# Two layers on one core: the first two columns of two projections made in turn, and two of the last four down blocks of the first MLP turned back by VectorE

## The chip, the core and the metric

The kernel runs on one core of a Trainium2 chip. A core has a matrix engine (TensorE, PE in the profile, with its weight loads as PEld), a vector engine (VectorE, DVE), a scalar engine (ScalarE, ACT), GpSimd (POOL), and DMA queues, here issued by SyncE (SP). The engines run their own instruction streams and meet at semaphores. The metric is the device time of one execution in microseconds; lower is better.

## The reference, cut to what matters

256 tokens of width 2048 pass through two layers, all in float32. Layer 1 is a Mamba-2 branch and an attention branch, whose outputs are joined and projected, and an MLP with squared ReLU. Layer 2 is an attention branch of three kinds and a gated delta rule, merged by two gates, projected, and a second MLP.

```python
def hybrid_layer_2(x, ...):
    ...
    g_a, g_b = jnp.split(jax.nn.sigmoid(merge), 2, axis=-1)
    x = x + (g_a * (o_a @ w_pa) + g_b * (o_b @ w_pb)) @ w_o
    h = rms_norm(x, ln2_w)
    return x + jnp.square(jax.nn.relu(h @ w_up)) @ w_down
```

In layer 1 the output projection is a product of 2048 inputs, half of them attention (`w_out_att`) and half the gated, normed output of the state-space part (`w_out_ssd`); its MLP has the same form as the last line above, with 8192 hidden units.

## The kernel before

**Weights.** They stream from HBM in pieces of 128x2048 through a ring of four. Each piece is two units of 128x1024. ScalarE casts a unit to its high half (`w_hi`, `unit_hi`), VectorE takes the difference (`w_lo`, `unit_lo`), and there is room for four units (`UNITS`). ScalarE may cast a unit once TensorE has used the one four back (`unit_used`). `weight_order` lists the pieces; the pieces of a pair of columns made in turn are split as first half, first half, second half, second half (`turns`, `unit_order`).

**Columns.** Most projections keep x transposed (features by tokens) and make 128 output features, a column, at a time: k tiles of 128 inputs, for each a 512-wide product of the high weights with both halves of x and a 256-wide one of the low weights with the high half of x. `project` makes columns one after another, `column` takes k tiles in twos (`products_of_two`, lines 548 and 551), `column_pair` makes two columns in turn (lines 542 and 543 in `products`). Three banks of PSUM go round: `bank_free` waits until the bank's last user but two has been read (`bank_read`), column by column.

**The joined output of layer 1.** `project_out_att` makes the 16 columns A0 to A15 over the attention half, 8 k tiles each, while VectorE works on the gate; then 16 columns G0 to G15 over the gated half follow. VectorE adds each bank to x in two halves (`residual`, lines 1349 and 1352). The gated half comes in four pairs of tiles; line 1651 makes the low half of each (semaphore `gate_dve`), steps lo00, lo01, lo10 and lo11.

**The MLPs.** They are made by tokens: `up_blocks` and `down_blocks` make 128 tokens by 512 features in a bank (lines 558 to 560), for four quarters f of the hidden units with four blocks n each, eight units a block. VectorE turns the squared ReLU with 32x32 block transposes (`turn_up`, line 1675), and adds the down blocks in `x_toks` (line 1775). In the first MLP's last quarter TensorE turns each finished block back to features (`turned_back`, line 850, eight transposes of 128x128 in two banks, in the middle of the next block), VectorE adds it to x (`back_to_x`, line 1719), ScalarE and VectorE make the gained x for the next layer (`gained`, line 1360), and GpSimd adds squares (line 2857). In the second MLP's first quarter VectorE turns x to tokens (`turn_x`, line 1683).

**The merged output of layer 2.** The last merge columns are multiplied and added by VectorE (lines 1977 and 1981); ScalarE casts a pair of tiles (`merged_split`, line 2676) and VectorE makes its low half (line 1954, semaphore `merged_lo`), eight pairs in all. Then `project` makes the 16 columns W0 to W15 of `w_o`, 16 k tiles each.

Of the kernel before, what the change touches and what calls it, by code (L numbers as in the profile page):

```python
# [13 lines left out]
P = 128  # L14
D = 2048
# [204 lines left out]
def weight_order(t):  # L220
# [4 lines left out]
    def add(name, first, n, in_turns=False):  # L225
        if in_turns:
            turns.append(len(order))
        order.extend(t[name][first + i] for i in range(n))
# [38 lines left out]
    merge(MERGE_BEHIND)  # L267
    add("w_o", 0, KD)
    mlp("w_up2", "w_down2")
# [16 lines left out]
def build(nc, t_in, x_out, bias_rows, x_kept, decays_kept):  # L286
    with ExitStack() as ctx:
# [6 lines left out]
        def sem(name):  # L294
            return ctx.enter_context(nc.semaphore(name))
# [220 lines left out]
        merged_hi, merged_lo = sem("merged_hi"), sem("merged_lo")  # L516
        tok_turned = sem("x_turned")
        down_made, down_added = sem("down_first_tokens_made"), sem("down_added")
# [16 lines left out]
        def _(e):  # L535
# [304 lines left out]
            A = GATE["dve"]  # L840
            drain(project(KD, mix, 0, 8, (gate_dve, [A[f"lo{k // 4}{k // 2 % 2}"] for k in range(8)])))

# [37 lines left out]
            def down_blocks(m, f, hid):  # L880
# [3 lines left out]
                for n in range(D // BLOCK):  # L884
                    b = (4 * m + f) * (D // BLOCK) + n
                    back = m == 0 and f == 3
                    last = m == 1 and f == 3 and n == 3
                    if back and n >= 2:
                        e.wait_ge(back_added, 2 * (n - 1))
                    for k in range(KD):  # L890
                        if back and n > 0 and k == 8:
                            turned_back(n - 1)
                        if n == 0 and k % 4 == 0:
# [362 lines left out]
            drain(merge(MERGE_BEHIND))  # L1256
            drain(project(KD, hn2, 0, KD, (merged_lo, [k // 2 + 1 for k in range(KD)])))
            mlp(1, mix2, hn2)
# [5 lines left out]
        def _(e):  # L1264
# [429 lines left out]
            def up_blocks(m, f, hid):  # L1694
                nonlocal unit
                for n in range(D // BLOCK):
                    b = (4 * m + f) * (D // BLOCK) + n
                    for i in range(8):
# [10 lines left out]
                        if n > 0:  # L1709
                            if i in (1, 2):  # L1710
                                turn_up(b - 1, i - 1)
                            elif i == 4:
                                squared_lo(b - 1, hid)

            def back_to_x(n):
                b = 3 * (D // BLOCK) + n
                for half in range(2):
                    e.wait_ge(back_turned, 2 * n + half + 1)
                    e.tensor_tensor(pair(xT, 2 * n + half), pair(xT, 2 * n + half), psum[3 + 2 * (b % 2) + half][:, :],
                                    ALU.add).then_inc(back_added, 1)  # L1720

# [12 lines left out]
            def down_blocks(m, f, hid):  # L1734
                nonlocal unit
                for n in range(D // BLOCK):
                    b = (4 * m + f) * (D // BLOCK) + n
                    for i in range(8):
# [9 lines left out]
                        if m and f == 0 and n > 0 and i in range(2, 6):  # L1748
                            turn_x(n, i - 2)
                        if m == 0 and f == 3 and n > 0:  # L1750
                            if i == 5:
                                back_to_x(n - 1)
                            elif i > 5:
                                for t in range(4 * n + 2 * i - 16, 4 * n + 2 * i - 14):
                                    gained(t, "ln1", mix2)
# [381 lines left out]
            e.wait_ge(x_back, 32)  # L2137
            drain(project(16, 2, gained_residual("ln2", mix2)))
            mlp(1, hn2)
# [5 lines left out]
        def _(e):  # L2145
# [81 lines left out]

            def project_gathered(per_use, gain=None, dst=None):

# [8 lines left out]

                for t in range(KD):
                    for i in range(per_use):  # L2240
                        split_to(unit + UNITS)
                        unit += 1
                        if i == per_use - 1:
                            if t > 0:
                                finish(t - 1, use - 1)
                            if t == KD - 1:
                                finish(t, use)
                            use += 1
                        yield
# [577 lines left out]
            merged_split(7)  # L2827
            drain(project_gathered(2, "ln2", mix2))
            mlp(1, hn2)
# [265 lines left out]
```

## Time and profile before

| | |
|---|---|
| median of 3 runs | 2618.96 us (2618.95 to 2619.89) |
| the profiled execution's own time | 2619.45 us |
| its span, first to last instruction | 2617.6 us |
| mean granted clock of TensorE | 0.999 of full speed |
| TensorE busy | 2600.3 us |
| VectorE, ScalarE, GpSimd busy | 1864.2, 1307.9, 212.9 us |

The span lies inside the time; 1.85 us are around it. A share of busy time is an average over the whole program. What an edit is worth is read from the place where it is made: which engine waits there, and for what.

### The profile page before, as it was taken

Reading aid. Unit: us, or ns where it says so; the run is one execution under the profiler, and the core shown is the slowest. Engines: PE = TensorE matmul, PEld = TensorE weight load, DVE = VectorE, ACT = ScalarE, POOL = GpSimd, SP = SyncE. Lnnn points to the kernel's source line nnn. Section 1 sums busy time; section 2 is a strip of 40 time slices with the busy share of each in tenths; the row PEclk is TensorE's granted clock in tenths of the full one; section 3 lists DMA queues with packets and bytes.
Section 4 is the critical chain, followed back from the end, with each engine's and each line's share of the span. In section 5 each row is a group of like instructions: output and inputs, shape, how many; then the busy total and the mean of one; then the engine's idle time right before and its main releaser. Section 6 shows DMA issues by size and latency. Waiting matters only on the chain. (4 is left out here: it accounts for less than half of the span.)

```text
span 2617.6 us, 33824 instructions
## 1 busy us (share of the span) xinstructions
PE 2600.3 (99%) x13404; PEld 2207.0 (84%) x13404; DVE 1864.2 (71%) x2717; ACT 1307.9 (50%) x1823; POOL 212.9 (8%) x188
## 2 busy tenths in 40 slices
PE   9999999999999999999999999999999999999998
PEld 8788888888888888888888888888888888888887
DVE  7788797757658567786877767566678877585685
ACT  6545554534445345565555545455554354453453
POOL 4014010000000000130412300000100000000000
PEclk9999999999999999999999999999999999999999
DMA  7654555555555555576444333355555555555553
GB/s 266 164 216 167 188 177 184 202 193 188 199 189 181 209 191 195 181 264 235 145 146 144 114 128 129 129 211 178 206 196 204 194 184 204 184 186 209 187 199 129
DMA packets 68468, 483.87 MB, mean 185 GB/s; under 512 B 8039, under 2 KB 8183, under 8 KB 11224
## 3 DMA queue, kind: packets, MB, share of 16 engines
q1 hardware_dynamic: 65520, 467.43, 50.4%
q0 software_dynamic: 2272, 12.87, 1.7%
q8 instruction: 106, 1.74, 0.3%
q10 hardware_dynamic: 520, 1.43, 0.1%
q14 instruction: 50, 0.41, 0.0%
HBM read 475.38 MB, written 6.31 MB: 184 GB/s over the span
## 5 line engine op out<-in xcount | busy, mean ns | idle before, releaser
L1280 DVE TENSOR_TENSOR w_lo<-weight_ring,w_hi 128x1024 fp32r<-128x1024 f32 x882 | 1083.6, 1239 | 577.8 <-ACT w_hi L2158 573.7
L2158 ACT CAST w_hi<-weight_ring 128x1024 fp32r<-128x1024 f32 x884 | 917.1, 1048 | 713.6 <-PE bank L560 580.1
L548 PE MATMUL bank<-mix,w_hi 128*128 128x512 f32 x1776 | 566.8, 400 | 3.1 <-DVE mix L1651 1.2
L558 PE MATMUL bank<-w_hi,h 128*128 128x512 f32 x1056 | 411.7, 390 | 0.0
L558 PE MATMUL bank<-w_hi,mix 128*128 128x512 f32 x1056 | 411.2, 389 | 0.0
L559 PE MATMUL bank<-w_lo,h 128*128 128x512 f32 x1056 | 410.9, 389 | 0.0
L559 PE MATMUL bank<-w_lo,mix 128*128 128x512 f32 x1056 | 410.9, 389 | 0.0
L560 PE MATMUL bank<-w_hi,h 128*128 128x512 f32 x1056 | 410.9, 389 | 0.0
L560 PE MATMUL bank<-w_hi,mix 128*128 128x512 f32 x1056 | 410.8, 389 | 0.0
L551 PEld LDWEIGHTS bank<-mix,w_lo 128*128 128x128 f32 x1776 | 333.6, 188 | 78.7
L551 PE MATMUL bank<-mix,w_lo 128*128 128x256 f32 x1776 | 349.7, 278 | 0.0
L548 PE MATMUL bank<-h,w_hi 128*128 128x512 f32 x864 | 280.6, 406 | 0.0
L548 PEld LDWEIGHTS bank<-mix,w_hi 128*128 128x128 f32 x1776 | 271.4, 189 | 6.5 <-issue 1.7
L1675 DVE STREAM_TRANSPOSE arena<-arena 32x256 f32<-32x256 f32 x512 | 223.0, 436 | 24.1 <-ACT arena L2478 16.9
L558 PEld LDWEIGHTS bank<-w_hi,h 128*128 128x128 f32 x1056 | 198.2, 188 | 41.9 <-DVE w_lo L1280 0.7
L560 PEld LDWEIGHTS bank<-w_hi,mix 128*128 128x128 f32 x1056 | 198.2, 188 | 41.2
L560 PEld LDWEIGHTS bank<-w_hi,h 128*128 128x128 f32 x1056 | 198.2, 188 | 41.2
L559 PEld LDWEIGHTS bank<-w_lo,h 128*128 128x128 f32 x1056 | 198.2, 188 | 41.1 <-issue 0.2
L558 PEld LDWEIGHTS bank<-w_hi,mix 128*128 128x128 f32 x1056 | 198.2, 188 | 40.9
L559 PEld LDWEIGHTS bank<-w_lo,mix 128*128 128x128 f32 x1056 | 198.3, 188 | 40.9
L551 PEld LDWEIGHTS bank<-h,w_lo 128*128 128x128 f32 x864 | 162.3, 188 | 38.2
L551 PE MATMUL bank<-h,w_lo 128*128 128x256 f32 x864 | 170.2, 278 | 0.0
(377 smaller groups left out, 1998.4 us busy)
## 6 DMA issues: line engine op xcount, KB each, us to landing
weight_ring<-in_w_up SPq DMA_DIRECT2D x128, 1024.0 KB, 4.8
weight_ring<-in_w_down SPq DMA_DIRECT2D x128, 1024.0 KB, 4.8
weight_ring<-in_w_merge SPq DMA_DIRECT2D x32, 1024.0 KB, 4.7
weight_ring<-in_w_gdn SPq DMA_DIRECT2D x24, 1024.0 KB, 4.8
weight_ring<-in_w_papb SPq DMA_DIRECT2D x16, 1024.0 KB, 4.8
weight_ring<-in_w_o SPq DMA_DIRECT2D x16, 1024.0 KB, 4.8
weight_ring<-in_w_xbc SPq DMA_DIRECT2D x12, 1024.0 KB, 4.8
weight_ring<-in_w_q SPq DMA_DIRECT2D x8, 1024.0 KB, 4.8
```

The source lines that it names most:

```text
L548: e.matmul(bank[:, :], w_hi[:, unit_at % UNITS, o + j * P:o + (j + 1) * P], x[:, :, at + j * S:at + (j + 1) * S], start=first and j == 0, ...
L551: done = e.matmul(bank[:, 0:S], w_lo[:, unit_at % UNITS, o + j * P:o + (j + 1) * P], x[:, 0, at + j * S:at + (j + 1) * S], start=False, st ...
L558: e.matmul(out, x[:, 0, at:at + m], hi, start=first, stop=False)
L559: e.matmul(out, x[:, 0, at:at + m], lo, start=False, stop=False)
L560: return e.matmul(out, x[:, 1, at:at + m], hi, start=False, stop=last)
L1280: e.tensor_tensor(w_lo[:, i, :], ring[:, p % PIECES, half * UNIT:(half + 1) * UNIT], w_hi[:, i, :].bitcast(F32), ALU.subtract).then_inc(un ...
L1675: done = e.transpose(dst[:, :, :, 32 * r:32 * r + 32], src[:, :, :, 32 * q:32 * q + 32])
L2158: e.copy(w_hi[:, i, :], ring[:, p % PIECES, half * UNIT:(half + 1) * UNIT]).then_inc(unit_hi, 1)
```

## The change

Three places are edited. (A) G0 and G1 are made in turn, four k tiles of each at a time, after both banks and both weight units have been waited for. (B) In the first MLP's last quarter the first and second blocks are turned back by VectorE in 32x32 pieces (`turn_back`) into `turned_m`, in the first units of the next block; the third and fourth still by TensorE. (C) W0 and W1 are made by `column_pair`, two k tiles of each at a time, their pieces split in turn; VectorE and ScalarE read both columns once both are done.

```diff
@@ -265,7 +265,7 @@
     add("w_gz1", 0, 4)
     merge(MERGE_BEFORE)
     merge(MERGE_BEHIND)
-    add("w_o", 0, KD)
+    add("w_o", 0, KD, True)
     mlp("w_up2", "w_down2")
     return order, turns
 
@@ -514,7 +514,7 @@
         head_scaled, z_silu = sem("head_scaled"), sem("z_silu")
         merge_tanh, merge_mult, merge_gated = sem("merge_tanh"), sem("merge_multiplied"), sem("merge_gated")
         merged_hi, merged_lo = sem("merged_hi"), sem("merged_lo")
-        tok_turned = sem("x_turned")
+        tok_turned, back_made = sem("x_turned"), sem("down_blocks_turned")
         down_made, down_added = sem("down_first_tokens_made"), sem("down_added")
         back_turned, back_added = sem("down_turned_back"), sem("down_added_to_x")
         tok_squared, tok_gained, ln_loaded = sem("tokens_squared"), sem("tokens_gained"), sem("ln_rows_loaded")
@@ -838,7 +838,22 @@
                                     together(ssd_output(0), ssd_output(1)), ssd_gate()),
                   one_after_another(project(XBC_T + Z_T, hn), project_out_att()))
             A = GATE["dve"]
-            drain(project(KD, mix, 0, 8, (gate_dve, [A[f"lo{k // 4}{k // 2 % 2}"] for k in range(8)])))
+            gated = [A[f"lo{k // 4}{k // 2 % 2}"] for k in range(8)]
+            banks = []
+            for _ in range(2):
+                banks.append(bank_free())
+                use += 1
+            e.wait_ge(unit_lo, unit + 2)
+            for g in range(2):
+                for j in range(2):
+                    for k in range(4 * g, 4 * g + 4, 2):
+                        if j == 0:
+                            e.wait_ge(gate_dve, gated[k])
+                        done = products_of_two(banks[j], unit + j, k * P, mix, k * S, k == 0, k == 6)
+                    if g == 1:
+                        done.then_inc(unit_used, 1)
+            unit += 2
+            drain(project(KD - 2, mix, 0, 8))
 
             def turned_back(n):
                 b = 3 * (D // BLOCK) + n
@@ -883,13 +898,10 @@
                 nonlocal unit
                 for n in range(D // BLOCK):
                     b = (4 * m + f) * (D // BLOCK) + n
-                    back = m == 0 and f == 3
                     last = m == 1 and f == 3 and n == 3
-                    if back and n >= 2:
-                        e.wait_ge(back_added, 2 * (n - 1))
                     for k in range(KD):
-                        if back and n > 0 and k == 8:
-                            turned_back(n - 1)
+                        if m == 0 and f == 3 and n == 3 and k == 8:
+                            turned_back(2)
                         if n == 0 and k % 4 == 0:
                             e.wait_ge(up_lo, b + k // 4 + 1)
                         if k % 2 == 0:
@@ -1254,7 +1266,8 @@
             drain(delta_chain(0), delta_chain(1), one_after_another(rounds(NORM_TURNS[1]), vector_norms(1)),
                   one_after_another(gdn_projections(1), merge(MERGE_BEFORE)))
             drain(merge(MERGE_BEHIND))
-            drain(project(KD, hn2, 0, KD, (merged_lo, [k // 2 + 1 for k in range(KD)])))
+            column_pair(hn2, (merged_lo, [k // 2 + 1 for k in range(KD)]), 2)
+            drain(project(KD - 2, hn2))
             mlp(1, mix2, hn2)
             assert unit == UNIT_AT["end"] and use == USE["end"]
 
@@ -1712,12 +1725,27 @@
                             elif i == 4:
                                 squared_lo(b - 1, hid)
 
+            def turn_back(n, q):
+
+                b = 3 * (D // BLOCK) + n
+                if q == 0:
+                    e.wait_ge(down_added, 2 * (b + 1))
+                for r in range(4):
+                    src = x_toks[32 * r:32 * r + 32, :].rearrange("p (c n t w) -> p n t c w", c=2, n=D // BLOCK, t=4)
+                    dst = turned_m[n % 2][32 * q:32 * q + 32, :].rearrange("p (t c w) -> p t c w", t=4, c=2)
+                    done = e.transpose(dst[:, :, :, 32 * r:32 * r + 32], src[:, n, :, :, 32 * q:32 * q + 32])
+                done.then_inc(back_made, 1)
+
             def back_to_x(n):
                 b = 3 * (D // BLOCK) + n
                 for half in range(2):
-                    e.wait_ge(back_turned, 2 * n + half + 1)
-                    e.tensor_tensor(pair(xT, 2 * n + half), pair(xT, 2 * n + half), psum[3 + 2 * (b % 2) + half][:, :],
-                                    ALU.add).then_inc(back_added, 1)
+                    if n < 2:
+                        e.wait_ge(back_made, 4 * (n + 1))
+                        got = pair(turned_m[n % 2], half)
+                    else:
+                        e.wait_ge(back_turned, 2 * (n - 2) + half + 1)
+                        got = psum[3 + 2 * (b % 2) + half][:, :]
+                    e.tensor_tensor(pair(xT, 2 * n + half), pair(xT, 2 * n + half), got, ALU.add).then_inc(back_added, 1)
 
             def scaled_tokens(c):
                 last = D // BLOCK - 1
@@ -1748,6 +1776,8 @@
                         if m and f == 0 and n > 0 and i in range(2, 6):
                             turn_x(n, i - 2)
                         if m == 0 and f == 3 and n > 0:
+                            if i in range(1, 5) and n <= 2:
+                                turn_back(n - 1, i - 1)
                             if i == 5:
                                 back_to_x(n - 1)
                             elif i > 5:
@@ -2135,7 +2165,14 @@
             drain(merge(MERGE_BEHIND))
             merged_split(7)
             e.wait_ge(x_back, 32)
-            drain(project(16, 2, gained_residual("ln2", mix2)))
+            evacuate = gained_residual("ln2", mix2)
+            split_to(unit + UNITS + 2)
+            unit += 4
+            e.wait_ge(unit_used, unit)
+            for t in range(2):
+                evacuate(t, psum[use % 3], bank_read[use % 3])
+                use += 1
+            drain(project(KD - 2, 2, lambda t, bank, read: evacuate(t + 2, bank, read)))
             mlp(1, hn2)
             assert unit == made == UNIT_AT["end"] and use == USE["end"]
 
@@ -2225,7 +2262,7 @@
                         e.wait_ge(res_gathered, FOLDED * n_gathered + s - 2)
                 e.activation(dst, pair(xT, s), ACT.Square).then_inc(res_squared, 1)
 
-            def project_gathered(per_use, gain=None, dst=None):
+            def project_gathered(per_use, gain=None, dst=None, paired=False):
 
                 nonlocal unit, use, n_gathered
 
@@ -2236,7 +2273,12 @@
                     if t % 2:
                         gather(t // 2)
 
-                for t in range(KD):
+                if paired:
+                    split_to(unit + UNITS + 2)
+                    unit += 4
+                    use += 2
+                    finish(0, use - 2)
+                for t in range(2 if paired else 0, KD):
                     for i in range(per_use):
                         split_to(unit + UNITS)
                         unit += 1
@@ -2825,7 +2867,7 @@
                   one_after_another(gdn_projections(1), merge(MERGE_BEFORE)))
             drain(merge(MERGE_BEHIND))
             merged_split(7)
-            drain(project_gathered(2, "ln2", mix2))
+            drain(project_gathered(2, "ln2", mix2, paired=True))
             mlp(1, hn2)
             for c in range(2):
                 squares(D // BLOCK - 1, c)
```

**TensorE at A.** The first rows of G0 before; bank2 and bank0 are the banks of G0 and G1, the semaphores are those of `gate_dve`, `unit_lo` and `bank_read`.

```order
L548 MATMUL bank2<-mix,w_hi 128x512 [waits ssd_gate_dve,unit_lo_made,gemm_bank_read2]
L548 MATMUL bank2<-mix,w_hi 128x512
L551 MATMUL bank2<-mix,w_lo 128x256 x2
L548 MATMUL bank2<-mix,w_hi 128x512 [waits ssd_gate_dve]
L548 MATMUL bank2<-mix,w_hi 128x512
L551 MATMUL bank2<-mix,w_lo 128x256 x2
L548 MATMUL bank2<-mix,w_hi 128x512 [waits ssd_gate_dve]
```

The same place in the changed kernel.

```order
L548 MATMUL bank2<-mix,w_hi 128x512 [waits unit_lo_made,ssd_gate_dve,gemm_bank_read0,gemm_bank_read2]
L548 MATMUL bank2<-mix,w_hi 128x512
L551 MATMUL bank2<-mix,w_lo 128x256 x2
L548 MATMUL bank2<-mix,w_hi 128x512 [waits ssd_gate_dve]
L548 MATMUL bank2<-mix,w_hi 128x512
L551 MATMUL bank2<-mix,w_lo 128x256 x2
L548 MATMUL bank0<-mix,w_hi 128x512 x2
L551 MATMUL bank0<-mix,w_lo 128x256 x2
L548 MATMUL bank0<-mix,w_hi 128x512 x2
L551 MATMUL bank0<-mix,w_lo 128x256 x2
L548 MATMUL bank2<-mix,w_hi 128x512 [waits ssd_gate_dve]
```

Four k tiles of G1 have moved between k tiles 3 and 4 of G0, and the first matmul now waits for two banks.

**VectorE at B.** After the adds of the first block (L1775), before.

```order
L1775 TENSOR_TENSOR arena<-arena,bank 128x512 [waits down_added,unit_used]
L1280 TENSOR_TENSOR w_lo<-weight_ring,w_hi 128x1024 [waits unit_hi_made] x6
L1719 TENSOR_TENSOR arena<-arena,bank 128x512 [waits down_turned_back] x2
L1280 TENSOR_TENSOR w_lo<-weight_ring,w_hi 128x1024 [waits unit_hi_made]
L1360 SCALAR_TENSOR_TENSOR h<-arena,vecs,h 128x256 [waits gained_x_hi] x2
```

The same place in the changed kernel, where those lines are 1805, 1293, 1748 and 1373.

```order
L1805 TENSOR_TENSOR arena<-arena,bank 128x512 [waits down_added,unit_used]
L1293 TENSOR_TENSOR w_lo<-weight_ring,w_hi 128x1024 [waits unit_hi_made] x2
L1736 STREAM_TRANSPOSE arena<-arena 32x8x32 [waits down_added]
L1736 STREAM_TRANSPOSE arena<-arena 32x8x32 x3
L1293 TENSOR_TENSOR w_lo<-weight_ring,w_hi 128x1024 [waits unit_hi_made]
L1736 STREAM_TRANSPOSE arena<-arena 32x8x32 x4
L1293 TENSOR_TENSOR w_lo<-weight_ring,w_hi 128x1024 [waits unit_hi_made]
L1736 STREAM_TRANSPOSE arena<-arena 32x8x32 x4
L1293 TENSOR_TENSOR w_lo<-weight_ring,w_hi 128x1024 [waits unit_hi_made]
L1736 STREAM_TRANSPOSE arena<-arena 32x8x32 x4
L1293 TENSOR_TENSOR w_lo<-weight_ring,w_hi 128x1024 [waits unit_hi_made]
L1748 TENSOR_TENSOR arena<-arena 128x512 [waits down_blocks_turned] x2
```

Sixteen transposes stand between the weight splits of the second to fifth unit, and the add-back reads no bank.

**TensorE at C.** In the changed kernel, where the second half of W0 and then of W1 begins (bank1 and bank2 are their banks).

```order
L542 MATMUL bank2<-mix,w_hi 128x512
L543 MATMUL bank2<-mix,w_lo 128x256
L542 MATMUL bank1<-mix,w_hi 128x512 [waits unit_lo_made,merged_lo]
L543 MATMUL bank1<-mix,w_lo 128x256
L542 MATMUL bank1<-mix,w_hi 128x512
L543 MATMUL bank1<-mix,w_lo 128x256
L542 MATMUL bank2<-mix,w_hi 128x512 [waits unit_lo_made]
```

W1's ninth k tile, which waits for the fourth unit, comes two k tiles after W0's ninth; in the kernel before all of W0 stood ahead of W1's first.

## Rows read from the trace of the kernel before

**Rows 1.** The page, part 1: busy time, its share, instructions.

```profile
PE 2600.3 (99%) x13404; PEld 2207.0 (84%) x13404; DVE 1864.2 (71%) x2717; ACT 1307.9 (50%) x1823; POOL 212.9 (8%) x188
```

**Rows 2.** The waits of TensorE: total us, times, longest us.

```profile
PE bank L548 <- DVE mix L1651: 1.2, 1, 1.2
PE bank L548 <- DVE arena L1352: 1.0, 1, 1.0
PE bank L548 <- DVE mix L1954: 0.9, 1, 0.9
```

**Rows 3.** Timeline of PE, 353 to 361: start us, us, line, operation, idle before.

```profile
354.01 0.63 PE L548 MATMUL bank<-mix,w_hi 128*128 128x512 f32 x2
...
356.74 0.73 PE L548 MATMUL bank<-mix,w_hi 128*128 128x512 f32 x2 [1.18 <-DVE mix L1651]
...
359.44 0.73 PE L548 MATMUL bank<-mix,w_hi 128*128 128x512 f32 x2 [0.95 <-DVE arena L1352]
```

**Rows 4.** Timeline of DVE in the same stretch.

```profile
357.38 1.22 DVE L1280 TENSOR_TENSOR w_lo<-weight_ring,w_hi 128x1024 fp32r<-128x1024 f32 x1
...
358.96 0.42 DVE L1352 TENSOR_TENSOR arena<-arena,bank 128x256 f32<-128x256 f32 x1
```

**Rows 5.** Timeline of PE, 0 to 18.

```profile
9.44 0.50 PE L542 MATMUL bank<-mix,w_hi 128*128 128x512 f32 x1 [2.24 <-DVE mix L1360]
...
10.25 0.76 PE L542 MATMUL bank<-mix,w_hi 128*128 128x512 f32 x1
...
13.82 0.39 PE L542 MATMUL bank<-mix,w_hi 128*128 128x512 f32 x1
```

**Rows 6.** Two windows: busy of PE, PEld, DVE, ACT, POOL, then PEclk, DMA.

```profile
10.35:13.65 3.30, 3.30 (x10) 2.50 (x10) 3.11 (x6) 3.30 (x7) 0.00 (x0) 0.50 1.02 418
...
354.00:364.00 10.00, 7.87 (x44) 6.52 (x43) 9.78 (x17) 4.86 (x7) 0.00 (x0) 1.00 0.40 118
```

**Rows 7.** Timeline of PE, 1040 to 1046.

```profile
1043.55 0.39 PE L560 MATMUL bank<-w_hi,mix 128*128 128x512 f32 x1
...
1044.89 0.40 PE L559 MATMUL bank<-w_lo,mix 128*128 128x512 f32 x1
```

**Rows 8.** All groups of instructions: busy us, mean ns, idle.

```profile
L2158 ACT CAST w_hi<-weight_ring 128x1024 fp32r<-128x1024 f32 x884 | 917.1, 1048 | 713.6 <-PE bank L560 580.1 <-PE bank L551 115.2 <-DMA weight_ring<-in_w_k 6.1
...
L1683 DVE STREAM_TRANSPOSE arena<-arena 32x256 f32<-32x256 f32 x64 | 27.9, 436 | 1.0
```

**Rows 9.** Timeline of DVE, 1034 to 1058.

```profile
1036.95 1.23 DVE L1280 TENSOR_TENSOR w_lo<-weight_ring,w_hi 128x1024 fp32r<-128x1024 f32 x1 [1.49 <-ACT w_hi L2158]
...
1052.59 0.88 DVE L1360 SCALAR_TENSOR_TENSOR h<-arena,vecs,h 128x256 fp32r<-128x256 f32 x2
...
1055.31 1.92 DVE L1360 SCALAR_TENSOR_TENSOR h<-arena,vecs,h 128x256 fp32r<-128x256 f32 x2
```

**Rows 10.** Timeline of POOL in the same stretch.

```profile
1055.54 1.40 POOL L2857 TENSOR_TENSOR arena<-arena 128x512 f32<-128x512 f32 x1 [648.99 <-ACT arena L2226]
```

**Rows 11.** One window, a block of the down projection (its third).

```profile
1056.30:1079.00 22.70, 22.70 (x106) 18.88 (x105) 15.46 (x16) 11.10 (x15) 2.83 (x3) 1.00 0.53 187
```

**Rows 12.** Timeline of DVE, 1820 to 1832.

```profile
1822.37 0.41 DVE L1300 TENSOR_TENSOR arena<-arena,bank 128x256 f32<-128x256 f32 x1
...
1829.02 2.36 DVE L1280 TENSOR_TENSOR w_lo<-weight_ring,w_hi 128x1024 fp32r<-128x1024 f32 x2 [0.32 <-ACT w_hi L2158]
```

**Rows 13.** Timeline of PE, 1822 to 1836.

```profile
1822.76 0.62 PE L548 MATMUL bank<-mix,w_hi 128*128 128x512 f32 x2
...
1829.57 0.64 PE L548 MATMUL bank<-mix,w_hi 128*128 128x512 f32 x2
...
1835.15 0.63 PE L548 MATMUL bank<-mix,w_hi 128*128 128x512 f32 x2
```

**Rows 14.** Timeline of PE, a column pair at 1104 to 1114.

```profile
1105.38 0.40 PE L542 MATMUL bank<-h,w_hi 128*128 128x512 f32 x1
...
1113.15 0.40 PE L542 MATMUL bank<-h,w_hi 128*128 128x512 f32 x1
```

## The prediction

> **What bounds the kernel now.** I read the page first: TensorE is busy for 2600.3 us of the 2617.6 us span [rows 1], every other engine for 71% or less. So only two things can move the time by much: work taken from or given to TensorE, and the few microseconds in which it stands. The table of its waits comes next; three of its lines lie where the change is made: 1.2 us for L1651, 1.0 us for L1352 and 0.9 us for L1954 [rows 2]. Each place was then read on TensorE and VectorE side by side, in order of time.
>
> **Part A, the gated output (before the first MLP).** Column G0 of `w_out_ssd` begins at 354.01, does k 0 to 3, waits 1.18 us for the low half of k 4 and 5 (L1651), goes on at 356.74, and then G1 waits 0.95 us until 359.44 [rows 3]. The first wait is the one that the new order is built around: it puts k 0 to 3 of G1 (1.4 us of work) ahead of it. The second is not for data. What releases it is L1352, the second half of an evacuation. VectorE makes it at 358.96, behind a weight split that starts at 357.38 [rows 4] and its first half, L1349, so it ends at 359.38. The evacuation is that of the column before the last of the attention half (A14): three banks go round, G0 takes the bank of A13, G1 that of A14. The order shows what moved: in the new kernel the very first matmul of G0 waits for `gemm_bank_read0` as well, the bank of A14, because both banks are taken before any product is issued. Nothing on VectorE changes here, and from 357.38 to 359.38 it works without a break (1.22 + 0.42 us in these two rows, 0.4 for L1349), so that evacuation ends at 359.38 again. TensorE, which started G0 at 354.01, now stands from there to 359.44: 5.43 us, some 5.3 of it idle once the previous matmul has drained.
>
> The price: before, G1 started at 359.44, with G0 done. Now G0 starts at 359.44, and the pair has G0's eight k tiles more to do. Eight k tiles are half of the sixteen that lie between 1829.57 and 1835.15 [rows 13], so 5.58 / 2 = **2.79 us more**. Both old waits vanish in the new one; the gain of hiding them is not had. Queued behind the waiting matmul is only TensorE's own work; VectorE and ScalarE have what they need up to 359.38, since the sums of squares were sent before. VectorE is late with nothing next: it still owed the evacuations of A14 and A15, and having made them it now waits for G0.
>
> The idle stretch has a second price, the clock. At the start TensorE stood for 2.24 us before 9.44 [rows 5], and in the stretch from 10.35 to 13.65 the granted clock was 0.50, that is the lower level of 1.2 GHz, with TensorE busy all the time [rows 6]. Five k tiles took 13.82 - 10.25 = 3.57 us there [rows 5] against 5 x 0.353 = 1.77 at the full level (the pace is worked out in part C): 1.8 us lost. The waits of 1.18 and 0.95 us [rows 3] are not followed by such a fall (1.00 from 354 to 364 [rows 6]). An idle time of 5.3 us is over twice the one that was, so I take the fall for all but certain. Its size is open: at the start the clock fell 3.15 us after TensorE had stopped (9.44 - 2.24 = 7.20, to 10.35) and was low for 3.3 us. The same delay here would put the fall into the idle time (354.2 + 3.15 = 357.3) and leave 1.2 us of work at half speed, 0.6 us lost; a fall on resuming costs 1.8. I take the middle, **1.2 us**, and keep 0 and 1.8 as ends. The Trainium skill (TensorE: Matmul & The Clock Gate, Part 1) says that the throttled state is the default and that activity releases it; by that the fall is due here, and without it the sum would be 1.2 lower. The start of this trace agrees (0.50 after 2.24 us).
>
> **Part B, two of four blocks turned back by VectorE.** Around one `turned_back` (eight transposes, L850) TensorE has L560 at 1043.55 and L559 at 1044.89 [rows 7]. Without the transposes the two would be two matmul steps apart; a step is 2.72/12 = 0.227 us (a split each 1.23 + 1.49 = 2.72 us [rows 9], twelve matmuls a unit). So one costs 1.34 - 0.45 = 0.89 us, and two of them are **1.78 us less**, wholly on the path since TensorE is never idle in these blocks, 22.70 of 22.70 us in the third of them [rows 11].
>
> VectorE gets 16 transposes of 32x256 per block. The same form in the second MLP takes 436 ns [rows 8]: 7.0 us per block. The third block of this phase holds 15.46 us of VectorE work in 22.70 [rows 11]; with 7.0 it is 22.4 us, against 21.8 us for a block without its transposes (8 units of 2.72; a unit is 1.23 of split and 1.49 of idle [rows 9]). Step by step: a unit with four transposes takes 1.23 + 1.78 = 3.01 us against 2.72, four of them make VectorE 1.2 us late; add-backs, the gains (0.88 to 1.92 us a pair [rows 9]) and the block's two adds carry the lateness on to about 3 us at the end of the second such block. TensorE feels it beyond this: a split is wanted three units after it can begin, 3 x 2.72 less the cast of 1.05 [rows 8] and the split of 1.23, 5.9 us. So the transposes are hidden, price 0; were the cover gone, each microsecond over 5.9 would be one on TensorE. `turned_m` and `x_toks` are VectorE's own there, the wait for `down_added` is for its own add. The last two blocks keep their transposes and places.
>
> One rule speaks against the add-back, L1719, whose second operand moves from PSUM to SBUF. First the row: a pair of L1360 takes 0.88 us, and 1.92 when GpSimd adds at the same time, from 1055.54 for 1.40 us [rows 9, 10]. The Trainium skill (SBUF — State Buffer, "SBUF: two separate sides") says that a VectorE instruction with two SBUF inputs and a GpSimd one that reads SBUF exclude each other for a whole instruction. By that the new adds could be held up once by 1.4 us, 4.5 us late instead of 3, which is still hidden; it counts in the chance of rival 3.
>
> **Part C, the pair of `w_o`.** Before, W0 starts at 1822.76, stops for L1954 (0.87 us and a little), and W1 starts at 1829.57, W2 at 1835.15 [rows 2, 13]. Now W0's start also needs the bank read by L1300, 1822.37 + 0.41 = 1822.78 [rows 12]: 0.05 us. The pace of `column_pair`: 22 k tiles from 1105.38 to 1113.15 [rows 14], 0.353 us each (against 5.58/16 = 0.349). Its order alternates two k tiles, so the merged pairs are asked for at half the speed and L1954 is never late. But the weights are: the second half of W1's column is now wanted after 18 k tiles, 1822.8 + 6.36 = 1829.2, and it is the fourth unit of the pair. VectorE makes it at 1829.02, the first of two splits in 2.36 us, behind the last merged pair [rows 12], and ScalarE's cast ahead of it stands behind the same pair. It is there at 1830.2. So a wait of 1.0 us takes the place of the one removed. The 14 tiles left take 4.94, with 0.1 for the restart 1835.25, against 1835.15: **0.1 us more**. Ends: 1.0 less if the split came in time (32 x 0.353 = 11.3 from 1822.8), 0.6 more if it slips by half a split.
>
> **Sum.** +2.79 + 1.2 - 1.78 + 0.1 = +2.3 us on the profiled execution's own 2619.45 us (span 2617.6), which is 0.5 above the median of 2618.96; carried to the median: **2621.3 us**, 0.09% more. A measurement of this kernel tells about 0.2% from no change, 5.2 us, so this is no change by that bound.
>
> **Rivals.**
> 1. The change does in part A what its order aims at: the bank of A14 is free in time. For it: the data wait would indeed be covered. Against: the rows of VectorE are back to back. Then 1.18 + 0.95 go: -2.1 - 1.8 + 0.1 = -3.8, **2615.1 us**.
> 2. The clock stays low after the idle stretch for the whole pair of columns. Against it: at the start it came back after 3.3 us. Eight k tiles of each at half speed lose 5.58 us in place of 1.2: **2625.7 us**, slower. It decides from 4.1 us lost, 8.3 us of work at 1.2 GHz.
> 3. VectorE's lateness in part B passes 5.9 us. If a transpose took 0.7 us, 16 x 0.26 x 2 = 8.4 us would come on top of 3, 5.5 over the cover: +7.8, **2626.8 us**. Against it: 436 ns over 64 instructions of the same form.
>
> **How the numbers follow.** Forecast 0.73, its own range 2619.5 to 2622.5 (clock 0 to 1.8, C -1.0 to +0.6). Rival 1 0.14, rival 2 0.06, rival 3 0.03; a remainder of 0.04, half on each side of the bound. Slower by over 0.2%: 0.06 + 0.03 + 0.02 = 0.11; faster by over 0.2%: 0.02; within: 0.87. Forecast and rival 1 hold 0.87, so the range is **2614.8 to 2624.0**.
>
> **What would show it.** Part A: one wait of about 5.3 us on TensorE at 359.4, L1352 its releaser, none of L1651, and a granted clock of 0.5 for a while behind it. Wrong if TensorE starts G0 near 354. Part B: no L850 in the second and third blocks, no new wait of TensorE there, 32 transposes of 436 ns. Part C: no wait for L1954, one of about 1 us for the weight split at 1830. I am wrong if the time ends below 2617 or above 2624.

## The result, and the profile after it

| | median of the runs (range) | profiled execution: time, span, mean clock |
|---|---|---|
| before | 2619.27 us (2618.73 to 2620.06, 22 runs) | 2619.45 us, 2617.6 us, 0.999 |
| changed | 2622.97 us (2621.89 to 2624.92, 22 runs) | 2623.1 us, 2621.2 us, 0.997 |

The ratio is 1.0013, with a 95% interval of 1.0008 to 1.0019: the changed kernel is 3.7 us slower, which is within the 0.2% that the prediction counts as no change. The 22 runs on each side resolve it from zero all the same. The two profiled spans differ by 3.6 us, so the traces show the whole of it.

The busy row of TensorE and the lines of its waits that lie in the edited places (or changed beside them):

```profile
PE 2600.5 (99%) x13388; PEld 2207.4 (84%) x13388; DVE 1878.3 (72%) x2749; ACT 1307.5 (50%) x1823; POOL 213.7 (8%) x188
```

```profile
PE bank L548 <- DVE arena L1365: 5.3, 1, 5.3
...
PE bank L542 <- DVE mix L1373: 2.3, 1, 2.3
...
PE bank L542 <- DVE w_lo L1293: 0.6, 1, 0.6
PE bank L865 <- DVE arena L1805: 0.2, 1, 0.2
```

Against [rows 2], the waits for the gated low half (then L1651) and for the merged low half (then L1954) are gone, and so is the one for the second evacuation half as it was. One wait of 5.3 us stands in their place, for that same evacuation half (now L1365). TensorE's busy time is about the same as in [rows 1], although it has 16 matmuls fewer, the transposes of two blocks: so others must have become longer; part A shows which.

**Part A.** TensorE in order of time (start, duration, line and operation, count; in brackets the idle time before it and its releaser):

```profile
353.70 0.40 PE L551 MATMUL bank<-mix,w_lo 128*128 128x256 f32 x2
359.40 1.19 PE L548 MATMUL bank<-mix,w_hi 128*128 128x512 f32 x2 [5.30 <-DVE arena L1365]
...
360.82 1.05 PE L548 MATMUL bank<-mix,w_hi 128*128 128x512 f32 x2
...
362.10 1.06 PE L548 MATMUL bank<-mix,w_hi 128*128 128x512 f32 x2
...
363.38 1.06 PE L548 MATMUL bank<-mix,w_hi 128*128 128x512 f32 x2
...
364.66 0.85 PE L548 MATMUL bank<-mix,w_hi 128*128 128x512 f32 x2
...
365.57 0.63 PE L548 MATMUL bank<-mix,w_hi 128*128 128x512 f32 x2
...
366.29 0.62 PE L548 MATMUL bank<-mix,w_hi 128*128 128x512 f32 x2
...
367.68 0.63 PE L548 MATMUL bank<-mix,w_hi 128*128 128x512 f32 x2
```

The row at 367.68 is the first of the next column, G2. In the kernel before, G2 begins here:

```profile
362.33 0.63 PE L548 MATMUL bank<-mix,w_hi 128*128 128x512 f32 x2
```

VectorE beside it:

```profile
357.30 1.22 DVE L1293 TENSOR_TENSOR w_lo<-weight_ring,w_hi 128x1024 fp32r<-128x1024 f32 x1
358.44 0.41 DVE L1362 TENSOR_TENSOR arena<-arena,bank 128x256 f32<-128x256 f32 x1
358.88 0.42 DVE L1365 TENSOR_TENSOR arena<-arena,bank 128x256 f32<-128x256 f32 x1
...
366.48 0.42 DVE L1362 TENSOR_TENSOR arena<-arena,bank 128x256 f32<-128x256 f32 x1 [4.12 <-PE bank L551]
```

And the granted clock in stretches of 0.2 us, at its fall and at its release (the number after POOL's count):

```profile
358.20:358.40 0.20, 0.00 (x0) 0.00 (x0) 0.20 (x1) 0.20 (x1) 0.00 (x0) 0.78 0.00 0
358.40:358.60 0.20, 0.00 (x0) 0.00 (x0) 0.20 (x2) 0.15 (x1) 0.00 (x0) 0.50 0.00 0
...
365.00:365.20 0.20, 0.20 (x2) 0.11 (x1) 0.00 (x0) 0.00 (x0) 0.00 (x0) 0.66 0.87 369
365.20:365.40 0.20, 0.20 (x3) 0.16 (x2) 0.00 (x0) 0.00 (x0) 0.00 (x0) 1.00 1.16 492
```

The evacuation of A14 ends at 359.30, as it did in [rows 4] to within 0.1 us, and the pair starts behind it, at 359.40, where before only G1 did (359.44 in [rows 3]). The clock is at its lower level, 1.2 GHz, from 358.31 (a mean of 0.78 between 358.2 and 358.4 is 0.11 us at 1.00 and 0.09 at 0.50) to 365.14, that is for 6.8 us, of which 5.7 hold work. The first ten k tiles, two to a row, take 365.57 - 359.40 = 6.17 us; at the full level two k tiles take 366.29 - 365.57 = 0.72 us, and 0.70 in the rows behind, so ten are 3.5 us. The clock and the restart cost 2.7 us, of which 0.1 is the restart; G1 paid that 0.1 at the same place before. G2 begins 367.68 - 362.33 = 5.35 us later than before, in a program that ran 0.08 us ahead at the end of A15 (353.70 here, 353.78 before): part A costs 5.4 us. VectorE's idle 4.12 us at 366.48 is the same delay seen from the other side; it costs nothing.

**Part B.** Where the first of the four blocks ends, VectorE adds it at L1775 in the kernel before and at L1805 in the changed one. The line of each in that stretch (min/median/max in ns, then the first and the last start), before and then changed:

```profile
L1775 DVE TENSOR_TENSOR arena<-arena,bank x2: 678/678/679, 1032.7 to 1033.3; 128x512 f32<-128x512 f32 x2
```

```profile
L1805 DVE TENSOR_TENSOR arena<-arena,bank x2: 679/680/680, 1038.0 to 1038.6; 128x512 f32<-128x512 f32 x2
```

The changed kernel is 5.3 us behind here, and 3.53 us behind at the first matmul of the kv pair, just after the four blocks; again before, then changed:

```profile
1100.88 0.39 PE L542 MATMUL bank<-h,w_hi 128*128 128x512 f32 x1
```

```profile
1104.41 0.39 PE L542 MATMUL bank<-h,w_hi 128*128 128x512 f32 x1
```

So part B gave back 1.8 us. VectorE of the changed kernel in this phase, first by line (1035 to 1105), then in order of time, then one window with the same limits as [rows 11] (the program is about 4 us behind by then, so it is the third block less its end, and the end of the second):

```profile
L1736 DVE STREAM_TRANSPOSE arena<-arena 32x256 f32<-32x256 f32 x32 | 13.9, 436 | 0.5
...
L1748 DVE TENSOR_TENSOR arena<-arena 128x512 f32<-128x512 f32 x4 | 2.6, 684 | 0.0
L1748 DVE TENSOR_TENSOR arena<-arena,bank 128x512 f32<-128x512 f32 x2 | 1.3, 678 | 0.0
```

```profile
1043.44 1.77 DVE L1736 STREAM_TRANSPOSE arena<-arena 32x256 f32<-32x256 f32 x4
1045.24 1.23 DVE L1293 TENSOR_TENSOR w_lo<-weight_ring,w_hi 128x1024 fp32r<-128x1024 f32 x1
...
1084.53 1.27 DVE L1805 TENSOR_TENSOR arena<-arena,bank 128x512 f32<-128x512 f32 x2
1085.72 2.35 DVE L1293 TENSOR_TENSOR w_lo<-weight_ring,w_hi 128x1024 fp32r<-128x1024 f32 x2
1088.54 1.23 DVE L1293 TENSOR_TENSOR w_lo<-weight_ring,w_hi 128x1024 fp32r<-128x1024 f32 x1 [0.47 <-ACT w_hi L2195]
```

```profile
1056.30:1079.00 22.70, 22.70 (x102) 18.80 (x101) 22.32 (x34) 11.97 (x17) 1.40 (x1) 1.00 0.54 193
```

VectorE is busy for 22.3 of 22.7 us where it was for 15.5 [rows 11], and TensorE is still never idle. Two splits in a row without a gap (1085.72) are VectorE catching up; at 1088.54 it waits for ScalarE again.

**Part C.** TensorE around the pair of `w_o`, and VectorE beside it:

```profile
1826.24 0.39 PE L551 MATMUL bank<-h,w_lo 128*128 128x256 f32 x2
1826.59 0.47 PE L542 MATMUL bank<-mix,w_hi 128*128 128x512 f32 x1
...
1832.56 0.40 PE L542 MATMUL bank<-mix,w_hi 128*128 128x512 f32 x1
...
1833.66 0.50 PE L542 MATMUL bank<-mix,w_hi 128*128 128x512 f32 x1 [0.58 <-DVE w_lo L1293]
...
1838.70 0.64 PE L548 MATMUL bank<-mix,w_hi 128*128 128x512 f32 x2
```

```profile
1830.59 1.48 DVE L1984 SCALAR_TENSOR_TENSOR mix<-arena,mix 128x512 fp32r<-128x512 f32 x2
1832.38 3.50 DVE L1293 TENSOR_TENSOR w_lo<-weight_ring,w_hi 128x1024 fp32r<-128x1024 f32 x3 [0.31 <-ACT w_hi L2195]
```

A weight split takes the place of the merged low half as what TensorE waits for. Without a wait W0 would start at 1826.47 (0.23 behind 1826.24). From there to W2 it is 12.23 us, against 12.39 before (1822.76 to 1835.15, [rows 13]): 0.16 us less in these two profiles. The stretch before is not a fixed one, though: in `only_B`, where `w_o` is made as before, the wait for the merged half was 0.52 us instead of 0.87 and the stretch 12.02 us. Whether part C gains or loses 0.2 us is not shown.

In sum: A +5.4, B -1.8, C -0.2: +3.4 of the 3.6 us between the spans.

### The profile page after: what moved, and what is told of

It reads as the page before. It is cut to its first block and busy times, and to the rows that moved or that the text cites. A ratio compares the mean times of both kernels' runs of the same rounds, so it can differ in the third digit from the quotient of the medians.

```text
span 2621.2 us, 33824 instructions
## 1 busy us (share of the span) xinstructions
PE 2600.5 (99%) x13388; PEld 2207.4 (84%) x13388; DVE 1878.3 (72%) x2749; ACT 1307.5 (50%) x1823; POOL 213.7 (8%) x188
## 5 line engine op out<-in xcount | busy, mean ns | idle before, releaser
L548 PE MATMUL bank<-mix,w_hi 128*128 128x512 f32 x1744 | 558.6, 402 | 5.4 <-DVE arena L1365 5.3
L551 PE MATMUL bank<-mix,w_lo 128*128 128x256 f32 x1744 | 344.4, 279 | 0.0
```

The source lines that it names most:

```text
L548: e.matmul(bank[:, :], w_hi[:, unit_at % UNITS, o + j * P:o + (j + 1) * P], x[:, :, at + j * S:at + (j + 1) * S], start=first and j == 0, ...
L551: done = e.matmul(bank[:, 0:S], w_lo[:, unit_at % UNITS, o + j * P:o + (j + 1) * P], x[:, 0, at + j * S:at + (j + 1) * S], start=False, st ...
```

## The experiments

**The parts alone.** `undo_A` is the changed kernel with part A taken back; `only_A` the kernel before with part A alone; `only_B` is `undo_A` with part C taken back as well.

```diff
 undo_A, only_B:
-            for _ in range(2):
-                banks.append(bank_free())
...
-            drain(project(KD - 2, mix, 0, 8))
+            drain(project(KD, mix, 0, 8, (gate_dve, [A[f"lo{k // 4}{k // 2 % 2}"] for k in range(8)])))
 only_B also:
-    add("w_o", 0, KD, True)
+    add("w_o", 0, KD)
```

> The changed kernel with part A undone, B and C left. Theory 1: -1.8 (two transposed blocks) and -0.2 (the pair of w_o as its trace shows it), 2.0 us less than before, about 2617.3; VectorE is up to 3 us late in part B and no wait of TensorE shows it. Theory 2: B and C cost, so the time stays at 2622 or more. The old waits of 1.2 and 1.0 us are back.

> The kernel before with part A alone (G0 and G1 in turn). Theory 1 (the pair starts late and at 1.2 GHz): 2.8 us for the eight k tiles that now lie behind 359.4, and 2.6 us for the low clock seen in the profile of the changed kernel; 5.4 us more than before, about 2624.7, with one wait of 5.3 us. Theory 2 (the loss is made by the work that VectorE got in part B and by the pair of w_o): part A alone gives 2.1 us back, about 2617.2, and no wait of over 2 us there.

> The kernel before with part B alone. Theory 1: 1.8 us less than before, about 2617.5, 0.2 above the kernel with B and C. If the pair of w_o is worth nothing, the two are equal; if it costs 0.1, as I forecast, this one is 0.1 faster.

Measured, each against the kernel before in the same sitting (2619.18 us):

| kernel | median (range) | ratio, 95% | span |
|---|---|---|---|
| only_A | 2624.55 (2623.91 to 2628.08) | 1.002, 1.0011 to 1.0029 | 2622.2 |
| undo_A | 2617.94 (2617.12 to 2619.91) | 0.9996, 0.9987 to 1.0005 | 2616.3 |
| only_B | 2617.79 (2617.30 to 2619.81) | 0.9995, 0.9986 to 1.0004 | 2615.7 |

Part A alone costs 5.4 us, resolved from zero, and its trace repeats the long wait:

```profile
359.12 1.19 PE L548 MATMUL bank<-mix,w_hi 128*128 128x512 f32 x2 [5.32 <-DVE arena L1367]
```

The medians give part B alone 1.4 us, and part C nothing: 2617.94 with it, 2617.79 without. Both intervals take in 1, so by their times neither `undo_A` nor `only_B` is resolved from the kernel before. The traces settle part B: from the first matmul of G0 to that of the kv pair it is 746.87 us before, 745.08 in `only_B` and 745.06 in `undo_A`, 1.8 us less in both. The spans of the two differ by 0.6 us, which is not part C's: at the start of the program the clock was low for 6.8 us in the profile of `undo_A` and for 3.4 us in that of `only_B`, and at G0 `undo_A` was already 1.1 us behind.

**Is the clock a cost of its own?** `warm_18` gives TensorE matmuls without a use, ahead of the wait, into a bank that nobody reads there; `warm_9` half as many. They change nothing of what VectorE has to do first.

```diff
+            for _ in range(18):      # warm_9: range(9)
+                e.matmul(psum[3][:, 0:P], ones[:, :], ones[:, :], start=True, stop=True)
             banks = []
```

> The changed kernel with 18 products of ones into an unused bank between A15 and G0; they add no result. They fill most of the idle time and need no data. Theory 1 with the clock as a cost of its own: the wait for L1352 shrinks to under 1 us, G0 still starts at 359.4, the granted clock stays at 1.00, and the time falls by 2.6 us to about 2620.4. If the slow stretch behind 359.4 came from something else (cold operands, the pace of two columns in turn), the time stays at 2623. If the fillers themselves run past 359.4, it rises.

> The changed kernel with 9 fillers in place of the 18: 2.1 us of products of ones, then about 3.3 us of idle time before 359.4. If an idle time of that length lowers the clock as the 2.24 us at the start did, the granted clock is 0.5 behind 359.4 and the time is 2621 to 2623; if it does not, 2620.7 as with 18.

`warm_18` took 2620.75 us (2620.18 to 2621.43), ratio 1.0006 (0.9998 to 1.0015), 1.57 us above the kernel before in its sitting where the changed kernel is 3.70 above: 2.1 us less. The pair starts where it did, but at full speed:

```profile
353.88 4.18 PE L843 MATMUL bank<-ones 128*128 128x128 f32 x36
359.36 0.70 PE L548 MATMUL bank<-mix,w_hi 128*128 128x512 f32 x2 [1.30 <-DVE arena L1367]
...
360.13 0.63 PE L548 MATMUL bank<-mix,w_hi 128*128 128x512 f32 x2
```

`warm_9` took 2622.11 us (2619.74 to 2623.27), ratio 1.0011 (1.0002 to 1.0020). Its work ahead lasts 2.17 us and leaves 3.30 us of idle time:

```profile
359.19 0.81 PE L548 MATMUL bank<-mix,w_hi 128*128 128x512 f32 x2 [3.30 <-DVE arena L1367]
...
360.23 1.06 PE L548 MATMUL bank<-mix,w_hi 128*128 128x512 f32 x2
```

The clock falls here too, but later (359.63) and for less long (to 363.04). This profile is of an execution of 2621.39 us with a mean clock of 0.999; seven of the eleven took 2622.07 to 2623.27 at 0.997 or 0.998, so their clock was low for longer than it shows. By `warm_18` 2.1 (times) to 2.6 us (traces, in the table below) of part A's 5.4 us are the clock's, and the rest is the late start.

**What holds the pair?** `late_waits` asks for the bank and the weight of G1 only where G1 begins, so that G0 can do k 0 to 3. `gate_later` does the same and moves an evacuation ahead on VectorE: one more turn is yielded in the gate's generator before its second half, so that the bank of A14 is read first.

```diff
 late_waits:
             for g in range(2):
                 for j in range(2):
+                    if g == 0:
+                        banks.append(bank_free())
+                        use += 1
+                        e.wait_ge(unit_lo, unit + j + 1)
 gate_later as well (VectorE):
                     if g == 0:
                         turn_sums(1)
+                        yield
                     yield
```

> The changed kernel, but G1's bank and G1's weights are waited for ahead of G1's first product and no longer ahead of G0's. Theory 1 (the bank of A14 sets the time): G0 does k 0 to 3 from 354.0 on, TensorE then stands 4.0 us until 359.4, and two pairs of k tiles fewer are left behind it: 1.4 us less than the changed kernel if the clock falls as before (about 2621.5), 4.0 less if it does not (2619). If the intended order only lacked this, TensorE would stand for no more than 1 us there and the time would be 2616.

> The last one, and VectorE makes the split of G1 and the evacuation of A14 ahead of its second half of the gate work (one more turn of its schedule), so that the bank is free at about 355.8. Theory 1: G1's first four k tiles then run while the gate is finished (to about 359.5); two short waits of 0.4 and 1.6 us, clock at 1.00, G2 starts 0.6 us earlier than without part A: 0.6 less than the kernel with B and C alone, about 2617.3. If VectorE's whole load there is the bound and nothing can be hidden, the time equals that kernel's, 2617.9, or is above it, because lo10 comes 2.1 us later.

`late_waits` took 2621.03 us (2620.64 to 2621.93), ratio 1.0008 (0.9999 to 1.0017), 2.2 us above the kernel before in its sitting instead of 3.7. Four k tiles moved ahead of the wait, 1.4 us, no more; and the clock still fell:

```profile
359.34 1.22 PE L548 MATMUL bank<-mix,w_hi 128*128 128x512 f32 x2 [3.87 <-DVE arena L1365]
```

`gate_later` took 2617.12 us (2616.45 to 2618.85), ratio 0.9994 (0.9985 to 1.0002), the lowest of all:

```profile
355.47 0.73 PE L548 MATMUL bank<-mix,w_hi 128*128 128x512 f32 x2 [0.19 <-DVE arena L1365]
...
358.38 0.73 PE L548 MATMUL bank<-mix,w_hi 128*128 128x512 f32 x2 [1.25 <-DVE mix L1664]
```

Now TensorE waits for what part A is built around, the gated data, and the clock stays at 1.00. Is that the turn order, or the moved evacuation alone? `serial_gate_later` is `undo_A` with the same extra `yield`.

> VectorE's order as in gate_later (the bank of A14 free by 355.8), but G0 whole ahead of G1, as before the change; B and C kept. If the turn order is what uses the early bank, TensorE stands about 2.6 us for lo10 after G0's k 0 to 3, 1.4 us are lost against gate_later, and the clock may fall on top: 2618.5 to 2621. If the turn order is worth nothing and VectorE's order alone made the gain, the time is that of gate_later, 2617.1.

It took 2620.27 us (2619.10 to 2620.41), ratio 1.0003 (0.9994 to 1.0012). Each against the kernel before in its own sitting (+1.0 and -1.75), it is 2.8 us above `gate_later`:

```profile
358.78 1.22 PE L548 MATMUL bank<-mix,w_hi 128*128 128x512 f32 x2 [3.10 <-DVE mix L1649]
```

With the columns one after another the later gate becomes a wait of 3.10 us, behind which the clock falls. The turn order puts 1.4 us of G1's work into it and keeps the clock up. So the order is worth its place, but only with the bank free. Against the kernel before, the interval of `gate_later` still takes in 1: its 1.75 us lower median is not resolved, and about three quarters of it is what part B gives alone.

What each arrangement costs in part A can be read without the rest of the program, from the time at which G0 could begin (0.23 us behind the last row of A15) to the first matmul of G2:

| kernel | G0 could begin | G2 begins | between |
|---|---|---|---|
| before | 354.01 | 362.33 | 8.32 us |
| changed kernel | 353.93 | 367.68 | 13.75 us |
| only_A | 353.63 | 367.35 | 13.72 us |
| warm_18 | 353.88 | 365.00 | 11.12 us |
| warm_9 | 353.72 | 366.39 | 12.67 us |
| late_waits | 353.91 | 366.40 | 12.49 us |
| serial_gate_later | 354.12 | 364.55 | 10.43 us |
| gate_later | 353.72 | 361.42 | 7.70 us |

With the clock kept up the late start alone costs 11.12 - 8.32 = 2.8 us, and the low clock the other 2.6. The later gate without the turn order loses 2.7 us against `gate_later`, as the times say. `gate_later` is the only order that is shorter than the one before, by 0.6 us.

**How far does the cover in part B reach?** `three_back` is `undo_A` with the third block turned back by VectorE too, which leaves TensorE one block.

```diff
-                        if m == 0 and f == 3 and n == 3 and k == 8:
-                            turned_back(2)
...
-                            if i in range(1, 5) and n <= 2:
+                            if i in range(1, 5):
```

> Parts B and C without A, and the third block too is turned back by VectorE (the fourth is still TensorE's). If VectorE's lateness stays hidden there: 0.9 us less than with two blocks, about 2617.0. If its cover ends (it is about 3 us late behind the second block, and the third's gains would come later still, ahead of the boundary where TensorE waits for them), a wait for L1775's add or for the gains takes the 0.9 us back and more: 2618 to 2620.

> The kernel with three blocks on VectorE once more, for a second profile: its times lie in two groups, about 2618.8 and 2621.1, and the profile of the first group shows a wait of 2.1 us with the clock at 1.00. If the other group is the clock falling behind that wait, a profile at about 2621 has the same wait and a stretch of 0.5 behind it; if it is a second or longer wait, it shows that.

> The same kernel a third time, so that both groups are met: as in the last one.

`three_back` took 2620.79 us (2618.18 to 2621.40), ratio 1.0004 (0.9995 to 1.0013); the single runs of the same kernel under the two other names 2619.09 and 2619.16. TensorE, and VectorE beside it:

```profile
1103.09 1.09 PE L850 MATMUL bank<-const_mats,arena 128*128 128x128 f32 x8 [2.14 <-DVE arena L1788]
```

```profile
1098.81 1.21 DVE L1276 TENSOR_TENSOR w_lo<-weight_ring,w_hi 128x1024 fp32r<-128x1024 f32 x1
1099.94 1.90 DVE L1356 SCALAR_TENSOR_TENSOR h<-arena,vecs,h 128x256 fp32r<-128x256 f32 x2
1101.76 1.27 DVE L1788 TENSOR_TENSOR arena<-arena,bank 128x512 f32<-128x512 f32 x2
```

With two blocks the last `turned_back`, in the kv pair, waits 0.25 us for VectorE's add of the fourth block, as it did before the change; with three it waits 2.14 us (2.14, 2.14 and 2.13 in the three profiles), 1.9 us more for 0.9 us saved. VectorE is not late for a split, it is late for that add, which stands behind a split and a pair of gains. The times of `three_back` lie in two groups, around 2618.8 and 2621.1. All three profiles are of the lower group, at a clock of 1.00 from 1097 to 1113. The mean clock of each execution says more: it was 0.999 in four of the five lower ones (0.998 in the fifth) and 0.997 in four of the six upper ones (0.998 in two). In the profiles of all these kernels 3.4 us at the low level go with a mean of 0.998 or 0.999, 6.8 with 0.998 and 10.2 with 0.997. So the upper group had more time at the low clock. A fall behind the 2.14 us would fit, but no profile shows where it was, and that stays open.

## Why the prediction was right, and where its sizes were off

The forecast was 2621.3 us, the result 2622.97: within the stated range of 2614.8 to 2624.0 and on its side of the bound, but 0.5 us above the 2619.5 to 2622.5 that the likeliest case had for its own. That case is the one that happened, with its clock term twice as large as forecast. Of the 1.7 us between the two, 0.3 is the base (2618.96 from three runs, 2619.27 from 22).

- **Part A, mechanism: right, and shown.** It is the bank of A14 that starts the pair. `gate_later` frees the bank earlier and the long wait is gone; `late_waits` leaves it and keeps 3.87 us of it. The wait was 5.30 us where about 5.3 was forecast, the releaser the one named, and the late start costs 2.8 us by `warm_18`, where the prediction took 2.79 from [rows 13].
- **Part A, the clock: the term that was mis-sized.** Forecast 1.2 us with ends 0 and 1.8, measured 2.6. The step that failed is the one that took the length of the low stretch from the start of the trace (3.3 us, [rows 5, 6]) as fixed, and asked only when it would begin. It began in the idle time, as the lower estimate had it, though at 358.31 and not at 357.3; but it lasted 6.8 us, 5.7 of them over work, and so the cost passed the upper end of 1.8. Nor is a fall as certain as the prediction took it: the profile of `warm_9` has an idle stretch of 3.47 us at the start of the program with none behind it (below). The forecast was a change of +2.3 us, the spans show +3.6, 1.3 us more: the clock gives +1.4 of that and part C -0.3; the 0.2 left is less than the start of the program varies by (below).
- **Part B: right in size.** -1.8 measured, -1.78 forecast; 436 ns for each of the 32 transposes. The cover was sized by the wrong consumer: the prediction looked for splits that come too late, over 5.9 us, and what is felt first is the wait of TensorE's own transposes for a block's add. With two blocks that wait is what it was before (0.25 us), with three it decides. So the price of 0 was right, but not for the reason given. The Trainium skill (SBUF — State Buffer, "SBUF: two separate sides") gave a reason for which the add-back from SBUF might be held up by GpSimd: the four took 684 ns each, the two that still read PSUM 678. But GpSimd had no instruction beside any of the four (its adds lie at 1060.12, 1079.61 and 1081.89, the four at 1055.62 and 1077.38), so they do not test it.
- **Part C: right in kind, its sign open.** The wait for the split is there, 0.58 us instead of 1.0: from W0's first matmul to the one that waits it is 7.07 us, where the prediction had 7.4. The 14 k tiles behind it took 5.04 us, as forecast (4.94 and 0.1), and W0 started 0.12 us late instead of 0.05. Together -0.16 in place of +0.1 between these two profiles, which is less than the stretch before varies by.
- **Rivals.** 1 (the bank is free in time) is refuted for this kernel and is what `gate_later` makes of it: 2617.12 us, where the rival's sum gave 2615.1. 2 (the low clock lasts through the pair) would have needed 8.3 us of work at 1.2 GHz and got 5.7. 3 did not happen; `three_back` shows that VectorE's lateness can be felt.

## What to carry to other kernels

When work is interleaved to hide a wait, look at everything the interleaved group takes before its first instruction: a bank or a semaphore that only the second half needed becomes the start time of the whole. Asking for it later is worth only the work that then fits in front; the rest comes from having it free earlier, here by another order on VectorE. Price an idle stretch on TensorE by its length and by the clock behind it, and leave the upper end of that second term wide: here the same kind of stretch was followed by 0, 3.4 or 6.8 us at the low level. Work moved to an engine with slack is free up to the first consumer that waits for anything of that engine, which need not be the consumer of what was moved.

## What the runs showed of the hardware

I had expected a low clock to last about as long as at the start, 3.3 us. It lasted 3.4 us in some cases and 6.8 in others. Idle time of TensorE, then the time at 1.2 GHz, read from stretches of 0.2 us:

| where | idle | low clock |
|---|---|---|
| start, before | 2.24 us | 10.29 to 13.71, 3.4 us |
| start, undo_A | 3.30 us | 8.40 to 15.23, 6.8 us |
| start, warm_9 | 3.47 us | none |
| start, three_back_third | 3.69 us | 10.83 to 14.24, 3.4 us |
| serial_gate_later | 3.10 us | 358.64 to 362.06, 3.4 us |
| warm_9 | 3.30 us | 359.63 to 363.04, 3.4 us |
| late_waits | 3.87 us | 358.63 to 365.46, 6.8 us |
| changed kernel | 5.30 us | 358.31 to 365.14, 6.8 us |
| only_A | 5.32 us | 357.94 to 364.76, 6.8 us |
| warm_18, gate_later | 1.30 us, 1.25 us | none |
| three_back, in three profiles | 2.14 us | none |

The length of the idle time does not settle it. At the same place, the start of the program, with nothing edited ahead of it, 2.24 us was followed by 3.4 us at the low level, 3.30 us by 6.8, 3.47 us by none and 3.69 us by 3.4; and 2.14 us in the middle of the program by none. The rows of part A alone would have suggested that a longer idle time means a longer fall. The start is thus also a part that varies from profile to profile: `undo_A`, with 6.8 us at the low level there, reached G0 at 354.87, and the other profiles between 353.6 and 354.3. That is as much as the medians of some of these kernels differ by. The 18 matmuls of `warm_18` stand as 36 in the trace and took 4.18 us, 116 ns each record, without a break.
